# The first stage of a two-layer hybrid trunk: the norm's weight row spread by PE, one bias matmul for four heads, block 0 in halves, and dummy matmuls while x loads

## The reference, cut to what matters

```python
def rmsnorm(x, g):
    y = xf * lax.rsqrt(jnp.mean(xf * xf, axis=-1, keepdims=True) + EPS)
    return (y * g).astype(x.dtype)

for layer in range(DEPTH):                      # 2
    h = rmsnorm(x, g_mix[layer])
    u = h @ w_mix_in[layer]                     # 1024 x 3088, one projection for all mixers
    aq, ak, av, gq, gk, gv, gr, glr, c_in, c_b, c_c = split(u)
    att = dilated_attention(aq, ak, av, rel_bias)   # logits + rel_bias[rel_bucket(distance)]
    go  = gated linear attention of gq, gk, gv, glr; rmsnorm; * silu(gr)
    cv  = short_conv(c_in, c_b, c_c)
    x = x + concat(att, go, cv) @ w_mix_out[layer]
    h = rmsnorm(x, g_ffn[layer])
    x = x + (swiglu(h) on layer 0, top-2-of-8 experts on layer 1)
return rmsnorm(x, g_final)
```

## Time and profile before

| | us |
|---|---|
| median of 3 runs | 1433.6 |
| lowest and highest | 1432.38, 1433.8 |
| the profiled execution | 1433.79 |
| its span | 1432.0 |
| PE busy in it | 1394.3 |

### The profile page before, as it was taken

One profiled execution on the slowest core, in us unless ns is written; L12 is line 12 of the kernel. 1 busy time (PEld: TensorE's weight loads), 2 busy tenths in 40 slices (PEclk: granted clock), 3 DMA queues, 4 the chain that ended last, 5 costly groups with the idle time before them and its releaser, 6 DMA issues.

```text
span 1432.0 us, 32932 instructions
## 1 busy us (share of the span) xinstructions
PE 1394.3 (97%) x14890; PEld 816.7 (57%) x14890; DVE 340.7 (24%) x420; ACT 277.9 (19%) x353; POOL 21.1 (1%) x36
## 2 busy tenths in 40 slices
PE   6999899999999999999999999999999999999996
PEld 4998788888998833534543443453453353454343
DVE  4568555435566510010010001001001001000001
ACT  4454443323652300000000000001001000000001
POOL 1000000000000000000000000000000000000000
PEclk9999999999999999999999999999999999999998
DMA  6833555513736499999999999999999999999960
GB/s 229 301 119 137 206 197 196 191 59 119 273 119 233 165 366 387 392 377 382 402 375 379 405 385 365 393 400 365 392 396 373 385 397 374 383 397 378 376 252 32
DMA packets 140354, 431.36 MB, mean 301 GB/s; under 512 B 12346, under 2 KB 18778, under 8 KB 140096
## 3 DMA queue, kind: packets, MB, share of 16 engines
q1 hardware_dynamic: 138672, 424.01, 78.3%
q0 software_dynamic: 1552, 5.32, 1.1%
HBM read 427.19 MB, written 2.10 MB: 300 GB/s over the span
## 4 chain that ended last, share of the span: by engine, by line
PE 95%; DVE 2%; DMA 1%; ACT 1%; issue 1%; SPq 0%; POOL 0%; DVEq 0%; POOLq 0%; ACTq 0%
PE psum L1636 41%; PE psum L1663 20%; PE psum L1222 8%; PE psum L1224 8%; PE psum L1223 8%; PE psum L1646 2%; PE psum L1677 2%; PE psum L1394 1%; DMA raw<-in_w_mix_in 1%; DVE wlo L804 0%; DVE h L817 0%; PE psum L1609 0%; PE psum L1241 0%; PE psum L1610 0%; ACT whi L564 0%
## 5 line engine op out<-in xcount | busy, mean ns | idle before, releaser
L1636 PE MATMUL psum<-ring,xe 128*32 128x512 f32 (+1 forms) x5952 | 568.9, 538 | 0.0
L1636 PEld LDWEIGHTS psum<-ring,xe 128*32 128x32 f32 x5952 | 189.5, 110 | 345.0 <-issue 310.9
L1663 PE MATMUL psum<-ring,gT 128*32 128x256 f32 x5376 | 296.0, 379 | 0.6 <-ACT gT L737 0.6
L1663 PEld LDWEIGHTS psum<-ring,gT 128*32 128x32 f32 x5376 | 174.6, 110 | 125.8 <-issue 13.8
L1119 DVE TENSOR_TENSOR gate<-gate,psum 128x768 f32<-128x768 f32 (+1 forms) x32 | 27.3, 855 | 601.2 <-ACT gate L732 601.2
L804 DVE TENSOR_TENSOR wlo<-raw,whi 128x2048 fp32r<-128x2048 f32 (+1 forms) x67 | 147.4, 2229 | 52.4 <-ACT whi L564 52.3
L564 ACT CAST whi<-raw 128x2048 fp32r<-128x2048 f32 (+1 forms) x67 | 122.3, 1860 | 58.3 <-PE psum L1224 32.5
L1222 PE MATMUL psum<-whi,f_hi 128*128 128x512 f32 (+1 forms) x320 | 126.1, 394 | 5.8 <-DVE wlo L804 5.0
L1224 PE MATMUL psum<-whi,f_lo 128*128 128x512 f32 (+1 forms) x320 | 123.2, 385 | 0.0
L1223 PE MATMUL psum<-wlo,f_hi 128*128 128x512 f32 (+1 forms) x320 | 123.1, 385 | 0.0
L737 ACT COPY gT<-psum 128x768 f32<-128x768 f32 (+1 forms) x32 | 23.0, 720 | 453.7 <-PE psum L1646 453.7
(11 more groups left out here) (207 smaller groups left out, 837.6 us busy)
## 6 DMA issues: line engine op xcount, KB each, us to landing
ring<-in_moe_w SPq DMA_DIRECT2D x672, 512.0 KB, 5.9
raw<-in_ffn_w SPq DMA_DIRECT2D x33, 1024.0 KB, 6.1
raw<-in_w_mix_in SPq DMA_DIRECT2D x22, 1024.0 KB, 7.1
raw<-in_w_mix_out SPq DMA_DIRECT2D x8, 1024.0 KB, 5.0
raw<-in_w_mix_in SPq DMA_DIRECT2D x4, 544.0 KB, 5.4
x<-in_x SPq DMA_DIRECT2D x2, 512.0 KB, 5.1
bias_by_distance<-setup_bias POOLq DMA_DIRECT2D x1, 1024.0 KB, 5.1
bias<-bias_by_distance POOLq DMA_DIRECT2D x2, 512.0 KB, 7.4
```

The lines of the kernel that those rows point to most:

```text
L1636: ins = mm(banks(j)[o:o + 32, g, 0:2 * q].rearrange("p (i c) -> p i c", i=2), rows_[:, k * CAP + 32 * g:k * CAP + 32 * (g + 1)], w[:, kk, ...
L1663: ins = mm(bank[6 + g // 2][32 * q:32 * (q + 1), 256 * (g % 2):256 * (g % 2 + 1)], gT[:, a:a + 32], w[:, o:o + 256], start=j == 0 and n == ...
```

## The change

The weight row. SP no longer loads `g_row` replicated. POOL loads it to one partition (4 KB), and PE spreads it to 128 partitions with two matmuls of a row of ones against it, into PSUM banks 6 and 7. The first norm on DVE reads it there.

The bias. One matmul with the four heads as its four stationary columns replaces the four that had each head's value widened to 128 columns. ACT copies the 4 x 512 result to SBUF, as its first instruction, and POOL's store to DRAM repeats each head's row 128 times. `setup_wide`, its two fills and DVE's four copies go.

Block 0. Its load, its cast and its subtraction come in two halves of four k-tiles. PE does its 48 products for both tiles in parts, ordered by what is there first, ahead of blocks 1 and 2.

Dummy matmuls. DVE fills `warm`, and PE multiplies it by itself eight times ahead of the weight row's matmuls and four times behind the bias matmul; nobody reads the result.

The core of the diff:

```diff
@@ SP, in mixer(0) and at the start @@
+                    if l == 0 and i == 0:
+                        sp.dma_start(raw[raw_slot[0]][:, 0:4 * nc_]..., w[:, 0:4, c:c + nc_]).then_inc(raw_first, 16)
+                        sp.dma_start(raw[raw_slot[0]][:, 4 * nc_:8 * nc_]..., w[:, 4:8, c:c + nc_]).then_inc(raw_full[raw_slot[0]], 16)
+                        continue
-                if t == 0:
-                    row = g_mix[0]
-                    sp.dma_start(g_row[:], bass.AP(tensor=row.tensor, offset=row.offset, ap=[[0, P], [1, D]])
-                                 ).then_inc(first_gains, 16)
@@ POOL @@
+            pool.dma_start(g_row[0:1, :], g_mix[0:1, :]).then_inc(first_gains, 16)
+            pool.dma_start(setup_rel[0:REL_BUCKETS, 0:NH], rel_bias).then_inc(hot_loaded, 16)
             pool.dma_start(setup_hot[0:REL_BUCKETS + 1, :], onehot_in).then_inc(hot_loaded, 16)
-            pool.dma_start(setup_rel[0:REL_BUCKETS, 0:NH], rel_bias).then_inc(hot_loaded, 16)
...
-            pool.wait_ge(bias_sb, NH)
-            pool.dma_start(bias_dram, setup_bias[:]).then_inc(bias_stored, 16)
+            pool.wait_ge(bias_sb, 1)
+            pool.dma_start(bias_dram.rearrange("p (h s) -> h p s", h=NH),
+                           setup_bias[0:NH, :].rearrange("h (o s) -> h o s", o=1).broadcast_to([NH, P, 512])
+                           ).then_inc(bias_stored, 16)
@@ ACT @@
+            act.wait_ge(bias_ps, 1)
+            nc.scalar.copy(setup_bias[0:NH, :], bank[4][0:NH, :]).then_inc(bias_sb, 1)
             for t in range(NT):
                 norm_squares(0, t)
+            act.wait_ge(raw_first, 16)
+            nc.scalar.copy(whi[0][:, 0:1024], raw[raw_slot[0]][:, 0:1024]).then_inc(hi_first, 1)
             turn_hi(0, 0)
-            split(0)
+            act.wait_ge(raw_full[raw_slot[0]], 16)
+            nc.scalar.copy(whi[0][:, 1024:2048], raw[raw_slot[0]][:, 1024:2048]).then_inc(hi_ready, 1)
             turn_hi(0, 1)
@@ DVE @@
+                if i == 0:
+                    dve.wait_ge(g_ps, 1)
+                    nc.vector.scalar_tensor_tensor(h[:, t * D:(t + 1) * D], psum[:, 6 * 512:8 * 512], rs[:, t:t + 1],
+                                                   x[:, t * D:(t + 1) * D], ALU.mult, ALU.mult).then_inc(h_ready, 1)
+                    return
...
+            nc.vector.tensor_copy(warm[:]..., ones[:]... .broadcast_to([P, 4, P])).then_inc(warm_set, 1)
+            nc.vector.memset(setup_rel[REL_BUCKETS:REL_BUCKETS + 1, 0:NH], 1.0).then_inc(rel_set, 1)
-            nc.vector.tensor_copy(setup_wide[0:REL_BUCKETS, :]..., setup_rel[0:REL_BUCKETS, 0:NH]...).then_inc(rel_set, 1)
+            first = raw[raw_slot[0]]
+            dve.wait_ge(hi_first, 1)
+            nc.vector.tensor_tensor(wlo[0][:, 0:1024], first[:, 0:1024], whi[0][:, 0:1024].bitcast(F32),
+                                    ALU.subtract).then_inc(lo_first, 1)
+            dve.wait_ge(hi_ready, 1)
+            nc.vector.tensor_tensor(wlo[0][:, 1024:2048], first[:, 1024:2048], whi[0][:, 1024:2048].bitcast(F32),
+                                    ALU.subtract).then_inc(lo_ready, 1)
             turn_lo(0, 0)
-            split(0)
             turn_lo(0, 1)
             split(1)
             split(2)
-            for i in range(NH):
-                dve.wait_ge(bias_ps, i + 1)
-                nc.vector.tensor_copy(setup_bias[:, 512 * i:512 * (i + 1)],
-                                      bank[(0, 1, 2, 7)[i]][:]).then_inc(bias_sb, 1)
@@ PE @@
-                for i in range(NH):
-                    mm(bank[(0, 1, 2, 7)[i]][:], setup_wide[0:REL_BUCKETS + 1, i * P:(i + 1) * P],
-                       setup_hot[0:REL_BUCKETS + 1, :], start=True, stop=True).then_inc(bias_ps, 1)
+                mm(bank[4][0:NH, :], setup_rel[0:REL_BUCKETS + 1, 0:NH], setup_hot[0:REL_BUCKETS + 1, :],
+                   start=True, stop=True).then_inc(bias_ps, 1)
+            def spread_gains():
+                pe.wait_ge(first_gains, 16)
+                for j in range(2):
+                    ins = mm(bank[6 + j][:], ones[0:1, :], g_row[0:1, 512 * j:512 * (j + 1)], start=True, stop=True)
+                ins.then_inc(g_ps, 1)
+            def warm_up(n):
+                for _ in range(n):
+                    mm(bank[3][:], warm[:, 0:P], warm[:], start=True, stop=True)
...
+            pe.wait_ge(warm_set, 1)
+            warm_up(8)
+            spread_gains()
+            bias_by_distance()
+            warm_up(4)
             pe.wait_ge(consts_loaded, 16)
-            for t in range(NT):
-                turn_rows(0, t)
             mixer(0)
```

More of the change, by code:

```diff
@@ L215, in trunk @@
         setup_rel = place("setup_rel", 8, offset=base["bias0"] + 5 * 2048)
-        setup_wide = place("setup_wide", NH * P, offset=base["bias0"] + 6 * 2048)
-        setup_bias = place("setup_bias", NH * 512, offset=base["bias0"] + 4 * 2048 + 3 * 2048)
+        setup_bias = place("setup_bias", 512, offset=base["bias0"] + 4 * 2048 + 3 * 2048)
+        warm = place("warm", 512, F32R, offset=base["bias0"] + 9 * 2048)
         setup_masks = place("setup_masks", LEVELS * P, I32, offset=base["bias0"] + 4 * 2048 + 3 * 2048 + 4 * 2048)
@@ L1163, in _ @@
             nc.vector.memset(ones[:], 1.0).then_inc(ones_set, 1)
+            dve.wait_ge(ones_set, 1)
+            nc.vector.tensor_copy(warm[:].rearrange("p (n c) -> p n c", n=4),
+                                  ones[:].rearrange("p (n c) -> p n c", n=1).broadcast_to([P, 4, P])).then_inc(warm_set, 1)
+            nc.vector.memset(setup_rel[REL_BUCKETS:REL_BUCKETS + 1, 0:NH], 1.0).then_inc(rel_set, 1)
             nc.vector.memset(w_gate[0:32, :], 0.0).then_inc(ones_set, 1)
@@ L1296, in bias_by_distance, with first_values, part @@
                 pe.wait_ge(hot_loaded, 32)
-                pe.wait_ge(rel_set, 2)
-                for i in range(NH):
-                    mm(bank[(0, 1, 2, 7)[i]][:], setup_wide[0:REL_BUCKETS + 1, i * P:(i + 1) * P],
-                       setup_hot[0:REL_BUCKETS + 1, :], start=True, stop=True).then_inc(bias_ps, 1)
+                pe.wait_ge(rel_set, 1)
+                mm(bank[4][0:NH, :], setup_rel[0:REL_BUCKETS + 1, 0:NH], setup_hot[0:REL_BUCKETS + 1, :],
[8 more added lines that the diff above has]
+                    mm(bank[3][:], warm[:, 0:P], warm[:], start=True, stop=True)
+            def first_values():
+                def part(t, ks, f, w, first=False, last=False):
+                    for k in ks:
+                        ins = mm(bank[5][:, 256 * t:256 * (t + 1)], f[:, k * SEQ + t * P:k * SEQ + (t + 1) * P],
+                                 w[:, 256 * k:256 * (k + 1)], start=first and k == 0, stop=last and k == KD - 1,
+                                 skip_group_check=True)
+                    return ins
+                turn_rows(0, 0)
+                pe.wait_ge(hi_first, 1)
+                pe.wait_ge(hT_hi, 1)
+                part(0, range(4), f_hi, whi[0], first=True)
+                turn_rows(0, 1)
+                pe.wait_ge(lo_first, 1)
+                part(0, range(4), f_hi, wlo[0])
+                pe.wait_ge(hT_hi, 3)
+                part(1, range(4), f_hi, whi[0])
+                part(1, range(4), f_hi, wlo[0])
+                pe.wait_ge(lo_ready, 1)
+                for t in range(NT):
+                    pe.wait_ge(hT_hi, 2 * t + 2)
+                    part(t, range(4, KD), f_hi, whi[0])
+                    part(t, range(4, KD), f_hi, wlo[0])
+                for t in range(NT):
+                    pe.wait_ge(hT_ready, 2 * t + 2)
+                    ins = part(t, range(KD), f_lo, whi[0], last=True)
+                ins.then_inc(block_used, 1)
             def head(i):
@@ L1306, in mixer @@
                 b = BASE[l]
+                if l == 0:
+                    first_values()
+                    pe.wait_ge(bias_sb, 1)
                 for t in range(NT):
[L1308 to L1313 removed]
+                    if l:
+                        if t:
+                            turn_rows(2, t)
+                        by_token_parts(b, 8, 256, t, 5, 256 * t, 2 * l)
                     by_token([(b + 1, 4), (b + 2, 4)], 512, t, (4, 6)[t], 0, gr_ps)
[L1315 removed]
                 by_feature([(b + 3, 4), (b + 4, 4)], 272,
```

20 lines of the change are left out of this document (7 added, 13 removed).

## The result

| | before | after |
|---|---|---|
| median, us (lowest to highest, runs) | 1432.99 (1432.33 to 1433.80, 4) | 1452.42 (1450.46 to 1455.45, 4) |
| profiled execution, us | 1433.79 | 1450.46 |
| its span, us | 1432.0 | 1448.7 |

The changed kernel is slower: ratio 1.0137, 95% interval 1.0117 to 1.0157, or 19.4 us more, where 7.4 us less were forecast.

A forecast was written before the change was run, and what follows sets the result against it. PE was taken as the bound, busy 1394.3 of 1432.0 us. Its opening could shorten by 11.3 us, 4 given back because `h` waits for the bias sum: 1433.8 - 7.4 = 1426.4 us, range 1424.9 to 1430.0.

The forecast's parts named there:

- The sum of the opening: Time until PE starts the first feature product: 37.8 us in place of 45.25, so 7.4 us less.
- Weight row: POOL's 4 KB load, issued at 1.29 us, lands 5.6 us later, at 6.9.
- B: Time at which PE's bias matmul ends, from which the later steps count; taken as 10.5 us.
- `wlo` of block 2: DVE's chain through the subtractions for blocks 1 and 2 ends at B + 16.3.
- Feature product: PE reaches the first one after 11.0 us of blocks 1 and 2, at B + 27.3, or 37.8 us.
- The clock at block 2: PE's clock is high when block 2 arrives; the rival, low clock there, cost 1.4 us, 1427.8, chance 12%.
- What is hidden: Work costed at nothing: the warm-up matmuls, and the 1024 KB bias store going near B + 9 instead of 35.6.
- 5.8 us of slack: DVE finishes `wlo` of block 6 by B + 30.3; PE wants block 6 at B + 36.
- shares engines with blocks 3 to 5: The bias store runs beside these loads, none of which PE wants before B + 27; no cost given.
- The slower one: Rival: weight row or `setup_hot` lands late behind the weight blocks; 1434.5, or 1435.9 with low clock at block 2; 5%.
- A wait further down takes the place of those removed: Rival: a slot is reloaded late, PE stops at blocks 5 and 6 or later; 4.5 us given back, 1430.9; 8%.
- the 1 us that the prediction allowed: Sign of error: time from first feature product to the span's end not the same as before within 1 us.

The follow-up runs named there:

- kernel 6: Changed kernel with the bias sum in 128 rows, 32 per head, stored by four transfers repeating each row 4 times; 1424.38 us, ratio 0.9951 to the kernel before.
- kernel 9: Changed kernel with its one bias store reading rows 0, 32, 64 and 96 in place of 0 to 3; 1436.05 us, ratio 1.0032 to the kernel before.
- kernel 5: Changed kernel with its one bias store reading rows 0, 5, 10 and 15 in place of 0 to 3; 1423.65 us, ratio 0.9942 to the kernel before.
- kernel 7: kernel 6 with ACT's bias copy moved behind both squares and the first half of block 0's cast; 1424.31 us, ratio 0.9945 to the kernel before.
- kernel 10: kernel 7 without the four dummy matmuls behind the bias matmul; 1421.56 us, ratio 0.9927 to the kernel before.

## Why the prediction was wrong, point by point

**The sum of the opening was right.** Weight row: 6.9 forecast, 6.13 measured (landed in 4.8 us, not 5.6). B: 10.5 against 9.9. First `h`: B + 2.8 against B + 2.5. `f_lo` done: B + 11.65 against B + 11.1. `wlo` of block 2: B + 16.3 against B + 15.6. Feature product: B + 27.3 against B + 26.7 in kernel 6, where nothing disturbs it. The gain: 7.4 forecast, 7.9 in kernel 6. The matmuls of the weight row took 1.98 us where 2 x 0.86 = 1.72 had been taken from the 33-row ones, the bias matmul 1.85 where it was 1.71. Part of that lies in the split of the 4.43 us, since three of 0.86 and one of 1.71 make only 4.29. The 0.77 us between the squares' end and `h` is 0.87 in the trace of before (5.69 to 6.56). The clock at block 2 was high, as chosen. That it was high for the weight row too was in part luck: it was so in seven of the ten profiles with dummies, and in the other three B would have been some 1.8 us later.

**The step that failed is in "What is hidden".** It says: "The bias store reads one row per head and repeats it, still 1024 KB", and costs it at nothing, as company of blocks 3 to 5 with 5.8 us of slack. The text has the very fact that decides, and counts bytes instead. With 5.1 us, which the store of before took, it would have been true. But that store read 128 partitions, the new one reads four neighbours 128 times. By the four forms run, it takes

| partitions read | ports, by the Trainium skill's formula | landing, us |
|---|---|---|
| 0 to 3 | 1 | 45.7 |
| 0, 32, 64, 96 | 2 | 26.0 |
| 0, 5, 10, 15 | 4 | 16.8 |
| 128 | 16 | 8.8 from first issue to last landing (four transfers, 6.2 each in the median) |

From four ports to two adds 9.2 us, from two to one 19.7: about 7 us, and 38 us divided by the number of ports, which is 1 MB at some 27 GB/s through one. This is an estimate from the first three rows. For 16 ports it gives 9.4; the four transfers of kernel 6 took 8.8 together, but the one store of before took 5.1, so the 7 us are no constant. No row of before had a transfer that repeats few partitions, so its cost was unknown and had to be bounded from both sides; a row that is slow for its bytes was at hand (`consts`, 74 KB in 12.0 us), and was used for the weight row only.

**The second half of the step: "shares engines with blocks 3 to 5".** Sharing was given no price. In fact the two 544 KB blocks took 13.9 and 37.2 us, where their median was 5.0 in kernel 6. So a slack of 5.8 us met a delay of some 32. Block 4 landed only when the store was nearly done: ACT took it at 60.58 us and POOL was released by the store at 63.92, in kernel 9 it was 43.20 and 44.48, in kernel 5 33.13 and 34.09. Why a block suffers so, I can only argue: it is complete with its last part, and some part of it lies behind the store's packets on the engines that carry them, or has to pass the same port. With the store on four engines and on 16 the wait was the same (26.2 and 26.7 us); with 16 block 3 was held too, and both blocks took 39.4 us (median). No run separates the two causes, so this one stays open.

**The rivals.** The slower one had 5% and put the delay on the weight row behind the weight blocks, at 1434.5; the weight row was early. "A wait further down takes the place of those removed" had the kind right, PE waiting for a late block, but it put the wait at blocks 5 and 6 or later, by DVE's pace, and at 4.5 us; it was block 4, by a transfer, and 26.2. Neither knew of the store.

**From 17.8 us to the end.** The feature product starts 17.8 us later, the span is 16.7 longer, the medians differ by 19.4. From the feature product to the end the profiled executions took 1386.8 us before and 1385.7 after, so 1.1 less, just beyond the 1 us that the prediction allowed; in kernel 6 it was 1385.2. What gives back this microsecond was not looked for. The medians add the scatter between executions, 5 us after. Against kernel 6 the change lost 26.4 us at the feature product (63.05 against 36.66), of which the new wait is 26.2.

## What to carry to other kernels

A transfer has a source as well as a destination: when a change replaces data that lie in many partitions by few rows that are read again and again, price it by which partitions it reads, not by its bytes alone, and if it must be, let the producer write the rows into partitions that are spread (here PE did it in 2.04 us in place of 1.85). A slow transfer can be paid for by others, here by weight blocks on another queue, so look for the victim among the loads under way beside it. And when work is taken off the front of one engine, look at what stands next in the queue of the one it feeds: kernel 7 gained nothing, and kernel 10, one line further, had the feature product 3.2 us sooner (33.01 against 36.24), though about half of that was the clock.
